# State space layer: power zero from memory, flips on ScalarE, alternated columns, four fewer constant products

## The reference, cut to what matters

```
u = rms_norm(x) @ w_in
a_bar = exp(lam * dt);  b_bar = ((a_bar - 1) / lam)[..., None] * b_mat
bu = einsum('tbgh,gph->tbgp', u, b_bar)
a_cum, s = associative_scan((a_elems, bu));  s = s + a_cum * h0
y = einsum('tbgp,ghp->tbgh', s, c_mat).real          # complex, real part
y = y + d_skip * u;  g = gelu(y);  val, gate = split(g @ w_glu)
h = x + val * sigmoid(gate)
```

## Time and profile before

| | us |
|---|---|
| three runs | 2037.36, 2034.41, 2035.9 |
| median | 2035.9 |
| profiled execution, its own time | 2034.78 |
| its span | 2033.0 |
| TensorE busy | 1966.4 (97%) |
| VectorE busy | 1381.4 (68%) |
| ScalarE busy | 865.5 (43%) |

### The profile page before, as it was taken

One profiled execution on the slowest core, in us unless ns is written; L12 is line 12 of the kernel. 1 busy time (PEld: TensorE's weight loads), 2 busy tenths in 40 slices (PEclk: granted clock), 3 DMA queues, 4 the chain that ended last, 5 costly groups with the idle time before them and its releaser, 6 DMA issues.

```text
span 2033.0 us, 24999 instructions
## 1 busy us (share of the span) xinstructions
PE 1966.4 (97%) x9434; PEld 1559.6 (77%) x9434; DVE 1381.4 (68%) x2046; ACT 865.5 (43%) x1342; POOL 253.9 (12%) x231
## 2 busy tenths in 40 slices
PE   7999999999999999999999999898999998999997
PEld 5787888888888776788888887687777776876665
DVE  7996476546645449657635654988888888437986
ACT  4574243222233348643222323444443444236773
POOL 3040100000010000010000001233333332000002
PEclk9999999999999999999999999999999999999999
DMA  7455323232233220032233223221222213322012
GB/s 225 109 140 151 100 85 105 81 114 94 85 103 105 92 85 10 5 107 86 84 108 107 93 78 94 83 63 52 78 84 73 80 61 101 96 82 72 28 32 78
DMA packets 79623, 178.33 MB, mean 88 GB/s; under 512 B 17680, under 2 KB 31248, under 8 KB 79504
## 3 DMA queue, kind: packets, MB, share of 16 engines
q1 hardware_dynamic: 75792, 169.92, 27.2%
q0 software_dynamic: 3424, 6.23, 1.2%
q10 hardware_dynamic: 288, 0.59, 0.1%
HBM read 169.43 MB, written 7.27 MB: 87 GB/s over the span
## 4 chain that ended last, share of the span: by engine, by line
PE 70%; DVE 18%; ACT 5%; issue 5%; DMA 1%; SPq 0%; POOL 0%; DVEq 0%; POOLq 0%; ACTq 0%
PE psum L430 16%; PE psum L433 16%; PE psum L431 16%; DVE wl L401 2%; PE psum L471 2%; PE psum L474 2%; PE psum L472 2%; PE psum L855 1%; PE psum L857 1%; PE psum L856 1%; ACT wh L390 1%; PE psum L452 1%; DVE mE L1654 1%; PE psum L455 1%; DVE mE L1673 1%
## 5 line engine op out<-in xcount | busy, mean ns | idle before, releaser
L401 DVE TENSOR_TENSOR wl<-raw,wh 128x1024 fp32r<-128x1024 f32 (+3 forms) x337 | 391.9, 1165 | 326.9 <-ACT wh L390 326.4
L430 PE MATMUL psum<-xh,wh 128*128 128x512 f32 x1368 | 541.6, 396 | 1.3 <-DVE mbc L1531 0.9
L433 PE MATMUL psum<-xh,wl 128*128 128x512 f32 x1368 | 533.7, 390 | 1.3 <-DVE wl L401 1.3
L431 PE MATMUL psum<-xl,wh 128*128 128x512 f32 x1368 | 532.9, 390 | 0.0
L390 ACT ACTIVATE wh<-raw 128x1024 fp32r<-128x1024 f32 (+3 forms) x337 | 315.5, 938 | 272.9 <-PE psum L433 168.5
L430 PEld LDWEIGHTS psum<-xh,wh 128*128 128x128 f32 x1368 | 257.0, 188 | 61.5 <-DVE mbc L1531 3.4
L433 PEld LDWEIGHTS psum<-xh,wl 128*128 128x128 f32 x1368 | 256.8, 188 | 56.7 <-DVE wl L401 2.9
L431 PEld LDWEIGHTS psum<-xl,wh 128*128 128x128 f32 x1368 | 257.0, 188 | 55.1 <-issue 2.6
L578 POOL TENSOR_TENSOR rs<-rs,sq 128x512 f32<-128x512 f32 x41 | 54.2, 1322 | 1087.8 <-ACT sq L563 1087.6
L431 PE MATMUL psum<-fl,wh 128*128 128x512 f32 x352 | 137.0, 389 | 0.0
L433 PE MATMUL psum<-fh,wl 128*128 128x512 f32 x352 | 137.0, 389 | 0.0
(11 more groups left out here) (500 smaller groups left out, 3355.4 us busy)
## 6 DMA issues: line engine op xcount, KB each, us to landing
raw<-d_w SPq DMA_DIRECT2D x224, 512.0 KB, 3.5
raw<-d_w SPq DMA_DIRECT2D x32, 384.0 KB, 3.1
raw<-d_w SPq DMA_DIRECT2D x48, 256.0 KB, 2.6
raw<-d_w SPq DMA_DIRECT2D x32, 320.0 KB, 2.9
Mt<-d_kd SPq DMA_DIRECT2D x64, 64.0 KB, 2.4
bc<-d_bc SPq DMA_DIRECT2D x8, 256.0 KB, 3.3
d_ud<-ust SPq DMA_DIRECT2D x8, 256.0 KB, 3.2
U<-d_ud POOLq DMA_DIRECT2D x64, 32.0 KB, 2.9
```

What stands on the lines that cost most here:

```text
L401: dve.e.tensor_tensor(K.wl[n % NH][:, 0:COLS[n]], K.raw[n % RAW][:, 0:COLS[n]], K.wh[n % NH][:, 0:COLS[n]].bitcast(F32), ALU.subtract).the ...
L430: pe.e.matmul(b[:, :], WH[:, o:o + P], XH, start=(k == k0), stop=False)
L431: pe.e.matmul(b[:, :], WH[:, o:o + P], XL, start=False, stop=False)
L433: mm = pe.e.matmul(b[:, :], WL[:, o:o + P], XH, start=False, stop=(k == k1 - 1))
```

## The change

- The flips of both tables go from VectorE to ScalarE. They stand in the item `prep` 5 of ScalarE's queue, after a wait for VectorE's `prep` 5 and ahead of `dense` 3. The signs of the upper half are turned in both tables, and the two constant matrices of `swap` and `state` change places to match.
- `CA`'s lag 0, which is the out-projection itself, is no longer computed: ScalarE's queue issues two DMAs for each set (`load_zero_act`, 64 partitions each), six of them between `prep_act` 2 and `prep_act` 3 and two after each of the copies `near` 0 to 4. `inC` goes over 8 lags and not 9. Both `combine` items wait for these DMAs on the same semaphore as for `bc`.
- The eight products of `near` alternate between the two groups of output partitions (0 to 15 and 32 to 47).
- `BUSY_TURN` is 2 and 2 for the first two sets in place of 5 and 3.

```diff
-BUSY_TURN = (5, 3, 0, 1, 0, 0, 1, 1)
+BUSY_TURN = (2, 2, 0, 1, 0, 0, 1, 1)
-def flip(K, dve, z, n, s0, s1):
...
+def flip(K, act, z, n, sign):
+
+    keep = K.CA[2][UP, :, 16:16 + 8 * n].rearrange("p a (j k) -> p a j k", k=n)
+    real, imag = (z[UP, c, :, :].rearrange("p (a j) k -> p a j k", a=8) for c in range(2))
+    own(K, act, "act", act.e.activation(keep, real, ACT.Copy))
+    own(K, act, "act", act.e.activation(real, imag, ACT.Copy, scale=sign))
+    act.e.activation(z[LOW, 1, :, :], z[LOW, 1, :, :], ACT.Copy, scale=-1.0)
+    act.e.activation(imag, keep, ACT.Copy, scale=sign).then_inc(K.S["pa"], 1)
...
+    if i == 5:
+        act.wait_ge("pd", 5)
+        flip(K, act, K.cb, 8, -1.0)
+        act.wait_ge("pa", 8)
+        flip(K, act, K.pw, 9, 1.0)
...
-    if i == 6:
-        dve.wait_ge("kdz", 128)
-        flip(K, dve, cb, 8, 1.0, 1.0)
     if i == 7:
-        dve.wait_ge("mat", 1)
         e.memset(K.quarter[:, :], math.pi / 2).then_inc(K.S["prep"], 1)
-        flip(K, dve, pw, 9, -1.0, -1.0)
...
-    c, n, b, dst = (K.cb, 8, 0, K.Bp) if i == 0 else (K.pw, 9, 2, K.CA[q % 3])
-    sh = [P, W, n, 16]
+    c, k, b, dst = (K.cb, 0, 0, K.Bp) if i == 0 else (K.pw, 1, 2, K.CA[q % 3])
+    sh = [P, W, 8, 16]
     bc = K.bc[q % 3]
-    dve.wait_ge(f"bc{q % 3}", 16 * (q // 3 + 1))
+    dve.wait_ge(f"bc{q % 3}", 48 * (q // 3 + 1))
     dve.wait_ge("mat", 2 * q + i)
+    dve.wait_ge("kdz", 128)
+    dve.wait_ge("pa", 8 + i)
...
-    for g in range(8):
-        j, i = g // 4, g % 4
+    pe.wait_ge(f"bc{q % 3}", 48 * (q // 3 + 1))
+    for n in range(8):
+        j, i = n % 2, n // 2
+        g = 4 * j + i
...
+def load_zero_act(K, act, q):
+
+    act.wait_ge("Kp", q - 2)
+    for half, c in ((LOW, 2), (UP, 3)):
+        act.e.dma_start(K.CA[q % 3][half, :, 0:16], K.d["bc5"][half, c, GS[q], :]).then_inc(K.S[f"bc{q % 3}"], 16)
...
     prep_act(K, act, 2)
+    for q in range(3):
+        load_zero_act(K, act, q)
     prep_act(K, act, 3)
...
+        elif what == "prep" and q == 5:
+            prep_act(K, act, 5)
...
         elif what == "near":
             near_act(K, act, q)
+            if q < 5:
+                load_zero_act(K, act, q + 3)
```

More of the change, by code:

```diff
@@ L1983, in own, with first_mul @@
     e.wait_ge(name, e.n)
-def first_mul(K, dve, out, x, y, t):
+def first_mul(K, dve, out, x, y, t, last=None):
     e = dve.e
@@ L1993, in first_mul @@
     own(K, dve, "dve", e.tensor_tensor(out[0], out[0], t[0], ALU.subtract))
-    own(K, dve, "dve", e.tensor_tensor(out[1], out[1], t[1], ALU.add))
-def flip(K, dve, z, n, s0, s1):
[L1999 to L2004, removed]
+    end = e.tensor_tensor(out[1], out[1], t[1], ALU.add)
+    if last:
+        end.then_inc(K.S[last], 1)
+    else:
+        own(K, dve, "dve", end)
+def flip(K, act, z, n, sign):
[5 more added lines that the diff above has]
+    act.e.activation(imag, keep, ACT.Copy, scale=sign).then_inc(K.S["pa"], 1)
 def prep_act(K, act, i):
@@ L2077, in prep_dve, with by_lag @@
         b8 = [s(j).unsqueeze(2).broadcast_to([P, G5, 8]) for j in (11, 0)]
-        first_mul(K, dve, (cb[:, 0], cb[:, 1]), (pw[:, 0, :, 0:8], pw[:, 1, :, 0:8]), b8, t)
-    if i == 6:
-        dve.wait_ge("kdz", 128)
-        flip(K, dve, cb, 8, 1.0, 1.0)
+        first_mul(K, dve, (cb[:, 0], cb[:, 1]), (pw[:, 0, :, 0:8], pw[:, 1, :, 0:8]), b8, t, "pd")
     if i == 7:
-        dve.wait_ge("mat", 1)
         e.memset(K.quarter[:, :], math.pi / 2).then_inc(K.S["prep"], 1)
-        flip(K, dve, pw, 9, -1.0, -1.0)
-def by_lag(t, n):
-    return t[:, :, 0:n * 16].rearrange("p g (k h) -> p g k h", h=16)
+def by_lag(t, k):
+    return t[:, :, k * 16:(k + 8) * 16].rearrange("p g (k h) -> p g k h", h=16)
 def combine(K, dve, q, i):
-    c, n, b, dst = (K.cb, 8, 0, K.Bp) if i == 0 else (K.pw, 9, 2, K.CA[q % 3])
-    sh = [P, W, n, 16]
+    c, k, b, dst = (K.cb, 0, 0, K.Bp) if i == 0 else (K.pw, 1, 2, K.CA[q % 3])
+    sh = [P, W, 8, 16]
     bc = K.bc[q % 3]
-    dve.wait_ge(f"bc{q % 3}", 16 * (q // 3 + 1))
+    dve.wait_ge(f"bc{q % 3}", 48 * (q // 3 + 1))
     dve.wait_ge("mat", 2 * q + i)
-    dve.e.tensor_tensor(by_lag(K.Bs, n), c[:, 0, GS[q], 0:n].unsqueeze(3).broadcast_to(sh),
+    dve.wait_ge("kdz", 128)
+    dve.wait_ge("pa", 8 + i)
+    dve.e.tensor_tensor(by_lag(K.Bs, 0), c[:, 0, GS[q], k:k + 8].unsqueeze(3).broadcast_to(sh),
                         bc[:, b].unsqueeze(2).broadcast_to(sh), ALU.mult).then_inc(K.S["dve"], dve.up())
@@ L2104, in combine @@
         dve.wait_ge("Yp", q - 2)
-    own(K, dve, "dve", dve.e.tensor_tensor(by_lag(dst, n), c[:, 1, GS[q], 0:n].unsqueeze(3).broadcast_to(sh),
+    own(K, dve, "dve", dve.e.tensor_tensor(by_lag(dst, k), c[:, 1, GS[q], k:k + 8].unsqueeze(3).broadcast_to(sh),
                                            bc[:, b + 1].unsqueeze(2).broadcast_to(sh), ALU.mult))
-    dve.e.tensor_tensor(by_lag(dst, n), by_lag(dst, n), by_lag(K.Bs, n), ALU.add).then_inc(K.S["mat"], 1)
+    dve.e.tensor_tensor(by_lag(dst, k), by_lag(dst, k), by_lag(K.Bs, 0), ALU.add).then_inc(K.S["mat"], 1)
 def busy_pe(K, pe, bank, n):
@@ L2195, in angles_made @@
 def angles_made(q):
-    return 7 + q if q < 2 else 5 + 2 * q
+    return 7 + 3 * q if q < 2 else 7 + 2 * q
 def angles_act(K, act, q):
@@ L2257, in swap_pe @@
     pe.wait_ge("V", q + 1)
-    pe.e.matmul(K.bank[7][:, :], K.five("mturn"), flat(K.V[q % 2]), start=True, stop=True).then_inc(K.S["turned"], 1)
+    pe.e.matmul(K.bank[7][:, :], K.five("turn"), flat(K.V[q % 2]), start=True, stop=True).then_inc(K.S["turned"], 1)
 def scan_dve(K, dve, q):
@@ L2281, in state_pe @@
     pe.wait_ge("S", q + 1)
-    pe.e.matmul(K.bank[0][:, :], K.five("turn"), flat(K.Ss), start=True, stop=True).then_inc(K.S["turned"], 1)
+    pe.e.matmul(K.bank[0][:, :], K.five("mturn"), flat(K.Ss), start=True, stop=True).then_inc(K.S["turned"], 1)
 def state_dve(K, dve, q):
```

## The result

| | us |
|---|---|
| changed kernel, median of 14 runs | 2040.66 (2037.79 to 2044.31) |
| kernel before, median of 14 runs beside it | 2036.85 (2033.72 to 2041.61) |
| ratio | 1.0019, 95% interval 1.0011 to 1.0026 |
| profiled execution after, its own time and span | 2038.56, 2036.8 |

The change costs 3.8 us. The interval reaches from 0.11% to 0.26%, so whether it lies beyond the 0.2% that the prediction named as its bound stays open; that it is slower does not. The time forecast was 2041.5 and the range 2036.5 to 2048. The forecast added 5.6 us to a kernel before of 2035.9; the measured kernel before ran at 2036.85, so the two times lie closer together (0.8 us) than the two costs (1.8 us).

The account below looks back on a forecast made before the run. VectorE's queue sets the pace up to near 0, TensorE's own work counts behind 94 us. Near 0 is 7.9 us late (5.5 + 2.4); savings and the ScalarE step leave +5.6, so 2041.5 us, range 2036.5 to 2048.

Parts of the forecast that it names:

- Flips ahead of the split: ScalarE's flips delay piece 5's high part; VectorE idles 6.3 us behind `prep` 5, `inB` 0 ends 4.35 us later.
- Fewer constant products: Before transposes 0: TensorE waits about 7.2 us, removed 3.6 us gain nothing, lower clock loses 1.7 us.
- The window at 1695 us: Earlier profile, 1695 to 1700 us: clock 0.66 behind 2.40 us idle, taken as 1.7 us of lost work.
- To near 0: Transposes 0 to near 0: 8.3 us of work plus 1.7 for the clock, near 0 at 66.8, +5.5 us.
- the start's term: Delay of VectorE's chain by the six DMA issues before ScalarE's Sin: 2.4 us, bounds 0 and 15.5.
- Alternated columns: Near's products alternating between output column halves save 0.41 us a near, bounds 0 and 0.75.
- Rival C: Alternating near's columns gains nothing: +8.5 us, 2044.4 us; chance 0.08.
- Lag 0 by DMA: Shorter `inC` saves 0.39 us a set on VectorE; ScalarE's 16 DMA issues take 0.5 us each.
- the step over ScalarE at near 1: Two DMA issues behind near 1 delay ScalarE's high part, and VectorE's low part waiting for it, by 1.0 us.
- The six issues at the start: Six DMA issues before ScalarE's Sin delay all of VectorE's chain by 2.4 us, bounds 0 and 15.5.
- Rival A: ScalarE's sequencer hides the six issues at the start, price 0 not 2.4: +3.2 us, 2039.1; chance 0.30.
- all of it arrives at the end: Nothing is changed behind 165 us, so the whole +5.6 us reaches the kernel's end.

Follow-up runs that it names:

- The first two experiments: Changed kernel with ScalarE's flips moved behind the high parts of pieces 5 and 6 (ratio 0.9973), then with only the `pw` flip moved back (1.0007).
- the first experiment: Changed kernel with ScalarE's flips moved behind the high parts of pieces 5 and 6: 2031.41 us, ratio 0.9973 to the kernel before.

## Why the prediction was right, point by point

- *Flips ahead of the split*: right in place and size. Expected 6.3 us of idle time on VectorE and +4.35 at `inB` 0; measured 6.58 and +4.1 (56.40 against 52.30). Eight flips took 5.45 us, with 5.2 expected. The first two experiments show this mechanism: it is what the forecast of a slower kernel rested on, and this part was not luck.
- *Fewer constant products*: right. The wait was 7.30 us, 7.2 expected; the loss by the clock 9.70 − 8.31 = 1.4 us, 1.7 expected. The window at 1695 us was a good measure for it.
- *To near 0*: +5.5 expected without the start's term, +5.0 measured. `inC` 0 was ready at 62.8, 3.4 us ahead of near 0, as said, so VectorE's saved `pw` flip bought nothing there.
- *Alternated columns*: 0.45 us a near and not 0.41. Rival C, no gain at all, came from the Trainium skill ("TensorE: Matmul & The Clock Gate", Part 3, what overlaps), by which a weight load overlaps with running products only when the row group differs. These records do not agree: with the same 128 rows throughout, alternating the column groups takes near from 1.50 to 1.05 us. But the five late nears gave 1.6 us (from +4.3 at transposes 3 to +2.7 behind near 7) and not 2.05: TensorE is not alone on the path there. Transposes 7 wait 1.06 us for VectorE where they waited 0.73.
- *Lag 0 by DMA*: the step over ScalarE at near 1 is right in place (VectorE waits 1.09 us for the high part before `inC` 2, not 0.76) and too dear: the two issues cost 0.4 us and not 1.0, because they too run beside the two copies of near, and ScalarE stood idle for only 0.28 us behind them. The prediction named a sign against this step, an idle time before transposes 3 that is not longer than before, and the changed kernel's profile has that sign: 0.78 us before, none after (98.20). There the second fall of the clock had made TensorE itself late. Where the clock held, the idle time was longer with ScalarE's issues (1.06 us with ten constant products, 1.14 in the first experiment) and as before with SyncE's (0.79), so the step stands in its smaller size.
- *The six issues at the start* is the step that failed: 2.4 us taken, nothing measured. Rival A was right in that, with its price (+3.2, 2039.1), and the measured +3.8 lies nearer to it than to the forecast of +5.6. The sequencer was ten instructions ahead, more than the eight that rival A spoke of. The row that I had read the price from shows how long an issue takes, not who waits for it. The sum was 1.8 us too high by four differences: −2.4 is this term; −1.0 lies between there and transposes 3 (5.3 reckoned without the start's term, 4.3 measured), about half of it at near 0 and the rest by the two issues behind near 1; +0.45 is what the five late nears fell short; and +1.1 comes behind near 7, where the prediction had nothing. That the last two make up for some of the first two is luck.
- *Behind near 7*: "all of it arrives at the end" did not hold in the profiles. The difference was +2.7 us at 160 us and +4.4 at the products that stand at 186.11 before and at 190.47 after, with longer waits of VectorE for transfers (1.29 us in place of 0.67, and 3.64 in place of 3.22); the span has +3.8. Whether the change or chance did this stays open.
- *The lower end of the range*: 2039.1, less 1.7 for the clock, less 7 × 0.09 for the nears, is 2036.8 and not 2036.5. Nothing hangs on it.
- *The second fall of the clock*, at transposes 2, stood in no step. It cost little, since VectorE was late for transposes 3 as well, and it isn't in every profile of these kernels: the first experiment and the one with ten constant products have the same wait of 1.85 us there and no fall, and the columns alone in the kernel before have one behind 2.23 us.

## What to carry to other kernels

Before moving work to an engine with time to spare, look at the instruction that comes next in its queue and at who waits for that: the moved work cannot start before its own input is there, and everything queued behind it then waits for all of it. ScalarE's 11 us of idle time lay ahead of that input; they were no room for 5 us of work that could only start when they ended and had VectorE's next high part behind it. A filler in front of a wait can be worth keeping for the clock until the wait is gone, even though it does no work (1.5 us from transposes 0 to near 0 here, not clear of noise in the timed runs). And in these traces the duration of a DMA issue was a price only where the engine itself had run dry; look for the work that its sequencer has already handed over.

## What the runs showed of the hardware

- ScalarE's sequencer issued six DMAs between 13.41 and 20.05 us while the engine was still working on instructions that stand before them in the program; an issue of 2.52 us delayed nothing that the profile shows (the Sin at 20.41 us, at 20.51 before and at 20.47 with SyncE's issues).
- Products with 16 columns of weights and all 128 rows take 1.50 us for 16 on one group of output columns after the other and 1.05 us when they alternate between two groups.
- The fall of TensorE's clock behind a wait is not the same each time: behind 7.30, 7.48, 7.24 and 4.61 us it fell to 1.2 GHz in all four profiles, behind 2.98 and 2.23 us it fell and behind 2.87 us it did not, and behind 1.85 us it fell in one profile and held in two others (the first experiment's and that with ten constant products). From transposes 0 to near 0 such a fall cost 1.4 us (changed kernel) to 2.8 us (old column order, 11.07 us in place of 8.31).
